# The scan phase of a hybrid diffusion layer on one core: state products as full 128x128 blocks, another order on GpSimd, eight tiles written out without a loop

## The reference, cut to what matters

```python
def wkv7_scan(r, w, k, v, kk, a, s0, reverse):
    def step(S, inp):
        r_t, w_t, k_t, v_t, kk_t, a_t = inp
        sa = jnp.einsum('bhij,bhj->bhi', S, -kk_t)
        S = (S * w_t[:, :, None, :] + sa[..., None] * (kk_t * a_t)[:, :, None, :]
             + v_t[..., None] * k_t[:, :, None, :])
        y = jnp.einsum('bhij,bhj->bhi', S, r_t)
        return S, y
    xs = tuple(jnp.swapaxes(t, 0, 1) for t in (r, w, k, v, kk, a))
    s_final, ys = lax.scan(step, s0, xs, reverse=reverse)
    return jnp.swapaxes(ys, 0, 1), s_final
```

## Time and profile before

| what | value |
|---|---|
| runs | 2868.01, 2872.29, 2879.94 us |
| median | 2872.29 us |
| the profiled execution | 2877.78 us, its span 2876.0 us |
| its mean granted TensorE clock | 0.922 |
| TensorE busy | 2554.9 us, 89% of the span |
| TensorE's weight loads | 1925.7 us, 67% |
| VectorE busy | 1799.1 us, 63% |
| ScalarE busy | 1247.8 us, 43% |
| GpSimd busy | 456.6 us, 16% |

### The profile page before, as it was taken

How to read it: one execution, slowest core, us unless ns; L and a number is a source line. 1 busy time by engine, 2 the same in 40 slices (tenths; PEclk the granted TensorE clock), 3 DMA queues, 4 the chain that set the end, 5 groups by cost and what they waited for, 6 DMA issues and landing times. The chain is left out here.

```text
span 2876.0 us, 55847 instructions
## 1 busy us (share of the span) xinstructions
PE 2554.9 (89%) x23700; PEld 1925.7 (67%) x23700; DVE 1799.1 (63%) x1920; ACT 1247.8 (43%) x1275; POOL 456.6 (16%) x438
## 2 busy tenths in 40 slices
PE   5999995888889988988789679999999999999993
PEld 4999993778778777788444446666666666666661
DVE  2344213755746647554214579898988888888884
ACT  2212212443534425433100066666666666666671
POOL 0000000431412414314002301101011101111111
PEclk8999996998988989889799789999999999999996
DMA  8453321000000000000441299999999999999983
GB/s 316 143 202 101 112 87 49 17 11 24 4 26 24 4 25 11 18 7 10 185 170 45 79 385 373 344 373 337 371 344 372 338 371 342 373 337 371 343 324 118
DMA packets 246221, 537.99 MB, mean 187 GB/s; under 512 B 13254, under 2 KB 53926, under 8 KB 245752
## 3 DMA queue, kind: packets, MB, share of 16 engines
q1 hardware_dynamic: 242936, 524.39, 49.5%
q0 software_dynamic: 3072, 10.49, 1.6%
HBM read 504.15 MB, written 30.70 MB: 186 GB/s over the span
## 5 line engine op out<-in xcount | busy, mean ns | idle before, releaser
L1738 DVE TENSOR_TENSOR w_lo<-w_raw,w_hi 128x4096 fp32r<-128x4096 f32 x192 | 866.7, 4520 | 117.6 <-ACT w_hi L1578 117.6
L1578 ACT ACTIVATE w_hi<-w_raw 128x4096 fp32r<-128x4096 f32 x192 | 695.7, 3624 | 126.8 <-PE ps_y L1677 87.7
L1675 PE MATMUL ps_h<-w_hi,xT_hi 128*80 128x512 f32 x1024 | 413.3, 404 | 34.7 <-DVE xT_lo L1769 26.8
L1676 PE MATMUL ps_h<-w_lo,xT_hi 128*80 128x512 f32 x1024 | 408.6, 399 | 0.0
L1677 PE MATMUL ps_h<-w_hi,xT_lo 128*80 128x512 f32 x1024 | 408.2, 399 | 0.0
L1675 PEld LDWEIGHTS ps_h<-w_hi,xT_hi 128*80 128x80 f32 x1024 | 154.4, 151 | 120.0 <-DVE xT_lo L1769 25.7
L1675 PE MATMUL ps_y<-w_hi,hiddenT_hi 128*80 128x512 f32 x512 | 204.6, 400 | 14.1 <-DVE hiddenT_lo L1796 14.1
L1677 PEld LDWEIGHTS ps_h<-w_hi,xT_lo 128*80 128x80 f32 x1024 | 154.5, 151 | 88.0 <-issue 5.1
L1676 PEld LDWEIGHTS ps_h<-w_lo,xT_hi 128*80 128x80 f32 x1024 | 154.7, 151 | 81.3 <-issue 4.6
L1676 PE MATMUL ps_y<-w_lo,hiddenT_hi 128*80 128x512 f32 x512 | 201.5, 394 | 0.0
L1677 PE MATMUL ps_y<-w_hi,hiddenT_lo 128*80 128x512 f32 x512 | 201.4, 393 | 0.0
(11 more groups left out here) (282 smaller groups left out, 4093.4 us busy)
## 6 DMA issues: line engine op xcount, KB each, us to landing
w_raw<-in_w_e SPq DMA_DIRECT2D x192, 2048.0 KB, 8.9
w_ada<-in_w_ada SPq DMA_DIRECT2D x6, 4096.0 KB, 17.8
w_in_raw<-in_w_in SPq DMA_DIRECT2D x23, 1024.0 KB, 6.2
rkv_scratch<-projected SPq DMA_DIRECT2D x24, 320.0 KB, 6.1
rkv_T<-rkv_scratch SPq DMA_DIRECT2D x8, 960.0 KB, 5.2
gates_scratch<-projected SPq DMA_DIRECT2D x16, 320.0 KB, 6.6
gate_sb<-gates_scratch SPq DMA_DIRECT2D x8, 640.0 KB, 6.2
x<-in_x_sample SPq DMA_DIRECT2D x8, 512.0 KB, 6.4
```

The costliest lines, as they stand in the source:

```text
L1578: act.activation(high_of[w][:, :, :], raw[w][s % 2][:, :, :], ACT.Copy).then_inc(s_hi[w], 1)
L1675: pe.matmul(out, x[0][:, k, :], w[0][:, k, ks], start=first, stop=False, skip_group_check=True)
L1676: pe.matmul(out, x[0][:, k, :], w[1][:, k, ks], start=False, stop=False, skip_group_check=True)
L1738: v.tensor_tensor(low_of[w][s % 2][:, :, :], raw[w][s % 2][:, :, :], high_of[w][:, :, :], ALU.subtract).then_inc(s_lo[w], 1)
```

## The change

- In `part`, kind "S", the four products of 64x64 blocks (two halves of the columns, for `Bt` with `U` and for `Kt` with `Vt`) become two products of the full 128x128 block. The off-diagonal blocks, which mix the two heads, are computed with them and never read.
- In GpSimd's body `t_start(b)` stands behind `m_off(b)` of the same group, where it stood behind the last group's `m_off`.
- `tiles` calls the body eight times with numbers, for all four compute engines, in place of the loop of three passes. SyncE's loop over tiles becomes one of the program that writes the kernel, so that its five passes stand one behind the other.

```diff
@@ tiles
-            body(0, 0, True, False)
-            with eng.Fori(0, (KD - 2) // 2) as j:
-                body(2 * j + 1, 1, False, False)
-                body(2 * j + 2, 0, False, False)
-            body(KD - 1, 1, False, True)
+            for i in range(KD):
+                body(i, i % 2, i == 0, i == KD - 1)
@@ block.sync
-            with sp.Fori(1, KD - 2) as i:
-
+            for i in range(1, KD - 2):
                 store_states(i - 1)
@@ block.gpsimd, body
                         tt_start(n)
                     m_off(b)
-                for b in range(NGR):
                     t_start(b)
                 for n in range(NGR, ND):
                     m_off(n)
@@ block.tensor, part
                         pe.wait_ge(s_us, at + dr + 1)
-                        for w, x in ((Bt[m][dr], U(dr, c)), (Kt[m][dr], Vt[m][:, c, :])):
-                            for hs in HALVES:
-                                last = pe.matmul(Sps[hs, hs], w[:, c, hs], x[:, hs], start=(w is Bt[m][dr]), stop=(w is Kt[m][dr]))
-                        last.then_inc(s_sn, 1)
+                        pe.matmul(Sps, Bt[m][dr][:, c, :], U(dr, c), start=True, stop=False)
+                        pe.matmul(Sps, Kt[m][dr][:, c, :], Vt[m][:, c, :], start=False, stop=True).then_inc(s_sn, 1)
```

## The result

The changed kernel takes 2846.3 us in the median of four runs (2843.91 to 2850.41), the kernel before 2874.36 us with one more run beside those shown (2868.01 to 2879.94): a ratio of 0.9905, 95% interval 0.988 to 0.9929. That is 28 us less, inside the forecast range (2834 to 2872) and faster by more than 0.5%. The forecast was 2856, 16.4 us less.

The account below looks back on a forecast made before the run. TensorE's row of work, with idle gaps and stretches at 1.2 GHz, was taken as the bound. Terms -12, -7, -5.4 and +8 sum to -16.4: 2861.4 us against the profiled execution, 2856 us as a median, range 2834 to 2872.

Parts of the forecast that it names:

- GpSimd's order, -12: Head of each tile's rounds: building T earlier removes TensorE's wait for it, 12 us less, bounds 0 and -18.
- The floor of VectorE: Second z-round: TensorE waits for VectorE's sum, so a tile like tile 1 wins only what VectorE wins, 0.7 us.
- Jumps, -7: Passages behind the loop's two jumps back: written-out tiles remove their added time, 7 us less, bounds -2.0 and -7.
- Registers, -5.4: Handoffs to TensorE in looped tiles: no register-computed wait values, 0.3 us at three handoffs in six tiles, 5.4 us less.
- State products, +8: Chain: full blocks cost 1.7 us a tile, less the second clock fall staying out in two of eight tiles; 8 us more.
- the second lower stretch: Chain between state steps 1 and 2: TensorE's clock falls to 0.50 for 6.00 us; forecast to stay out in two tiles.
- That rival, with 0.17: Chain: the second clock fall stays out everywhere through more work there, state term -10 instead of +8, 2838 us; chance 0.17.
- The clock stays down, 0.20: Chain: the clock rises later than behind the first four state parts, 7.2 us a tile, up to 2919 us; chance 0.20.
- the two signs of being wrong: A wait of 1 us or more on m_off in each tile, or a lower stretch in the chain longer than 10 us.

Follow-up runs that it names:

- the last experiment: The change with TensorE's program alone back in its loop, the other engines still written out: 2853.24 us, ratio 0.9941 to the kernel before.
- the order alone: The kernel before with only GpSimd's order changed, tiles still looped and state products still 64x64: 2855.9 us, ratio 0.9947.
- the small products with fillers: The change with 64x64 state products back and one unread 128x128 matmul behind each direction's part: 2893.9 us, ratio 1.0088 to the kernel before.
- one experiment: The change with two 128x128 filler matmuls at the head of tiles 1 to 7: 2858.86 us, ratio 0.9939 to the kernel before.

## Why the prediction was right, and where it was not

The bound was right: TensorE's row with its idle time and its clock, GpSimd's T at the head of the rounds, the jumps, the chain. The forecast was 9.7 us too slow: the sum of -16.4 was short of the measured -28 because the term of the state products had the wrong sign. That it was not further off is in part luck: the gain forecast for the registers was not there and made up for some of it, and what the clock gave in the rounds and in the chain through all parts together was in no term.

- **GpSimd's order, -12:** right in size, and in part by another way. Alone 16.9 us; in the change the rounds gave 14.5. The floor of VectorE was named and is real: first z to w_rate 15.16 us in tiles 1 to 6 (forecast 15.3), L1060 0.82 us (forecast 0.83). The wait for `m_off` was 0.46 us in these tiles, where none worth naming was forecast, and 1.83 us in the last, not 1.4. Tile 0, put at 0, waited 1.65 and 0.56 us for `m_off` and still had rounds 2.4 us shorter, since two falls of the clock were gone. What I didn't see is how far the floor reaches: up to the keys of the second direction, where the wait grew by 8.9 us. A tile with no fall has 77.5 us to its first X with the new order and 78.5 without it, so only 1.0 us a tile is time won directly. The rest of the 14.5 is falls of the clock that left the rounds, which I had priced in for tile 2 and in smaller sums for others.
- **Jumps, -7:** right: 5.6 in the heads and 2.0 of idle time ahead of them. It is TensorE's own jump, as the last experiment shows. That the added time behind the idle gap is lower clock was true of the kernel before, but with TensorE's loop alone it was a second idle gap. By the Trainium skill's 108 ns (Advanced Engine Details and Errata, Control Flow Timing) it would have been 0.2; the trace decided rightly.
- **Registers, -5.4:** a gain that was not there. The 0.28 us at the one place of the earlier trace rows was won exactly (1.82 to 1.54), but it stands ahead of VectorE's floor, and tiles without a fall in the rounds are equally long to the first X looped and written out (77.46 and 77.51 us, tile 4 of the order alone and of the change). The looped head is 0.3 us longer there, and the rounds take it back. I had multiplied a handoff by three without asking what bounds the stretch it lies in.
- **State products, +8:** wrong sign; the chain gave 12.7 without the jumps' idle time. The price of a part was near at the full clock (0.48 against 0.245, so 0.24; forecast 0.27), but of the 1.7 us a tile only 0.7 reach the path; a wait of 0.78 us for VectorE that the small products have behind the context's output, for one, is not there with the full ones. And the second lower stretch stayed out in eight tiles, not in two. That rival, with 0.17, was the right reading at -10; the blocks' own share is 5 to 8 by the experiments, and the rest came with the other parts through the clock. Its reason, more work in that stretch, is not borne out: other work of about the same length made it worse. The factor of two of the Trainium skill (TensorEngine Tiling (Array Packing), When to Use Tiling) holds for the parts themselves, which took 0.98 us for four as small ones and 1.93 as full ones, and decides nothing here. (Working the sum over with that factor gives an estimate of 2.8 us less over the scan, not the some 2 that I wrote.)
- **The clock stays down, 0.20:** it did not in this kernel, but the small products with fillers show that it does when the stretch is made otherwise, 9 us a tile and more than the 7.2 I had priced. Neither of the two signs of being wrong came: no `m_off` wait of 1 us in each tile, and the lower stretch in the chain is as long as it was.
- The range held the result with 12 us to spare at its lower end; the spread that the position of the tiles adds (10 to 13 us in one experiment) was not in its reasons.

## What to carry to other kernels

Where TensorE is the bound, read the granted clock tile by tile beside the waits: here waits of one or two microseconds cost themselves and often a stretch at 1.2 GHz behind them, and the second was the larger. Put work nobody needs into such a wait and see whether the stretch goes; here three matmuls a tile brought 31 us, the whole change 28. And measure edits of this kind together, not only apart: each of the three alone shortened the chain by 12 to 14 us, and all together by 14.7. Before you put such a gain down to an edit, shift the work by a small delay: 0.45 us a tile moved this kernel by 10 to 13.

## What the runs showed of the hardware

- Fillers of three 128x128 products in a wait of 0.92 us kept the clock at 1.00 for the 27 us behind it, in eight of eight tiles. Over all profiled kernels the clock fell at this place in 65 of 80 tiles without the filler and in none of 32 with it.
- Once down, the clock stayed down for 31 to 34 us at some 96% busy when 64x64 products alternated with single 128x128 ones, where it came back during the four state parts in the change and just behind them before.
- 0.45 us more work in a tile of 109.1 us made it 112.65, with falls that had not been there.
- A jump back on TensorE, behind a body of two tiles, cost 1.95 and 1.4 us of idle time with only TensorE looped, at a clock of 1.00.
- A handoff to TensorE took 1.82 us with all engines looped and 1.55 with only TensorE looped or none.
- An instruction of VectorE (L1067) took 1.18 us with GpSimd busy beside it and 0.82 with GpSimd idle.
